# The output projection's weight rests subtracted on GpSimd instead of VectorE

## The chip, the cores and the metric

The kernel runs on one core of a Trainium2 chip. A core has five engines that run side by side, each with its own order of instructions: TensorE multiplies matrices, VectorE and ScalarE work on rows of up to 128 partitions, GpSimd does general work and sums over partitions, SyncE issues transfers. They wait for each other through semaphores. The metric is the device time of one execution in microseconds, as the median of several.

## The reference

One layer of a decoder, for a prompt of 1024 tokens and for eight samples with one new token each, whose keys and values of 2048 earlier tokens lie in a cache of pages of 128. All in 32-bit floating point. The middle part is what matters here:

```
o = attend(q, k, v, lam)                      # differential attention, 4 heads
o = rmsnorm(o, subln_g) * (1 - lam_init)
pz, pool_state = pool(z)                      # causal pooling, windows 2/4/8/16
m = concatenate([o, pz]) @ w_out              # the output projection, 1024 x 1024
x = x + g1 * rmsnorm(m, post_mix_g)
```

For the samples, the attention weights are a softmax over the 2048 cached positions and the new one, in two halves per head: exp(l - max) / sum, and the second half is subtracted with the factor `lam`. Ahead of this stand the adaptive modulation and the input projection; behind it a router and 64 experts, of which each token uses eight.

## The kernel before

The program is a row of stages with a barrier between them. In the first (up to 344 us) the input is projected, and the scores of the samples against all 128 pages of cached keys are left in `sc`, 128 partitions by 1088 columns. The stage of interest runs from 344 to about 730 us; behind it come router and experts.

This stage has 32 items: 8 blocks of 128 prompt tokens by 4 heads (`s` = 4 `i` + `k`). Each engine runs through the items in an order written out by hand. For an item, TensorE makes the scores (L1278, L1282), VectorE takes the maxima (L1453), ScalarE the exponentials (L1089), VectorE combines the two softmaxes (L1462 to L1467), TensorE transposes (L1308), ScalarE copies out (L1098), TensorE multiplies with the values (L1317), and VectorE copies the result into `o_h` (L1475). The scores of item s+1 are made ahead of item s's transposes.

Two further things are woven into the first items.

*The samples' weights.* VectorE takes the maximum of `sc` over pages (L1586, semaphore `dmax`); GpSimd takes the maximum over partitions (L1070, `gmax`); in item 0 VectorE subtracts it (L1603) and ScalarE takes the exponential (L1196); in item 1 VectorE sums over pages (L1607, `dsum`); GpSimd sums over partitions (L1072, `gsum`); in item 2 VectorE makes the weights `wV` from this (L1527 to L1538). From item 3 on TensorE multiplies 11 pages of values per item with `wV` (L1295). The pages come through a ring of seven buffers, `vring`; SyncE issues a page once the page seven places ahead of it has been used.

*The output projection's weights.* The projection is done with three products of rounded numbers: each operand is split in a rounded part and a rest. `w_raw` (1024 x 1024, eight blocks of 128 x 1024) is loaded at the start of the stage. In items 0 to 3 ScalarE rounds two blocks each into `w_hi` (L1200, semaphore `w_hi_made`), and VectorE subtracts them into `w_lo` (L1613, `w_lo_made`), which lies in the place of `w_raw`. TensorE uses them for the first time in item 4 (L1339), behind a wait for all eight rests.

GpSimd has little else in this stage: behind the two sums over partitions it makes the 16 small biases of the norms (L1063, L1067), the first of them near 419 us.

Of the kernel before, what the change touches and what calls it, by code (L numbers as in the profile page):

```python
# [8 lines left out]
F32 = mybir.dt.float32  # L9
# [3 lines left out]
ALU = mybir.AluOpType  # L13
# [6 lines left out]
KC = D // P  # L20
# [149 lines left out]
def build(nc, ins, outs):  # L170
# [7 lines left out]
    with ctx:  # L178
# [3 lines left out]
        def place(name, kb, shape, dt=F32):  # L182

            return nc.alloc_sbuf_tensor_at(name, shape, dt, offset=base + int(kb * 1024))
# [3 lines left out]
        def sem(name, keep=False):  # L188
            s = nc.alloc_semaphore(name)
            if not keep:  # L190
                used.append(s)
            return s
# [667 lines left out]
        W_STEPS = 4  # L860
# [39 lines left out]
        w_raw = place("w_raw", 139, [P, KC, D])  # L900
        w_lo = place("w_lo", 139, [P, KC, D], F32R)
        w_hi = place("w_hi", 171, [P, KC, D], F32R)
# [13 lines left out]
        w_hi_made, w_lo_made = sem("w_hi_made"), sem("w_lo_made")  # L916
# [29 lines left out]
        with nc.Block() as block:  # L946
# [112 lines left out]
            @block.gpsimd  # L1059
            def _(pool):  # L1060
                def bias_m(i):
                    pool.wait_ge(ss_m, 2 * i + 2)
                    pool.tensor_scalar(s3[:, 2:3], s3[:, 1:2], 1.0 / D, EPS, ALU.mult, ALU.add).then_inc(m_bias, 1)  # L1063

                def bias_x(i):
                    pool.wait_ge(ss_x, 2 * i + 2)
                    pool.tensor_scalar(s3[:, 6:7], s3[:, 5:6], 1.0 / D, EPS, ALU.mult, ALU.add).then_inc(x_bias, 1)  # L1067

                pool.wait_ge(dmax, 1)
                pool.partition_all_reduce(dm[:, 1, :], dm[:, 0, :], P, RED.max).then_inc(gmax, 1)  # L1070
                pool.wait_ge(dsum, 1)
                pool.partition_all_reduce(dm[:, 3, :], dm[:, 2, :], P, RED.add).then_inc(gsum, 1)  # L1072
                for i in range(1, NT):
                    bias_m(i - 1)
                    if i >= 2:
                        bias_x(i - 2)
                bias_x(NT - 2)
                bias_m(NT - 1)
                bias_x(NT - 1)
# [366 lines left out]
            def _(dve):  # L1446
                own = Own(dve, dve2)

                def maxima(s):
                    i = s // NH  # L1450
                    for m in range(2):
                        dve.wait_ge(s_done[m], s + 1)
                        dve.tensor_reduce(s2[s % 4][:, m:m + 1],  # L1453
                                          ps[:, 2 * m:2 * m + 2, :].rearrange("p b t -> p (b t)")[:, 0:(i + 1) * P], AX_X,
                                          ALU.max, negate=True).then_inc(nmax_here[m], 1)

                def combine(s):

                    st_, n = s2[s % 4], (s // NH + 1) * P
                    for m in range(2):  # L1460
                        dve.wait_ge(exp_done[m], s + 1)
                    own(dve.reciprocal(st_[:, 4:6], st_[:, 2:4]))  # L1462
                    own.wait()
                    own(dve.scalar_tensor_tensor(out=st_[:, 6:7], in0=st_[:, 2:3], scalar=neglam[:, 0:1], in1=st_[:, 5:6],
                                                 op0=ALU.mult, op1=ALU.mult))
                    own.wait()
                    dve.scalar_tensor_tensor(out=ex2[s % 2][0][:, 0:n], in0=ex2[s % 2][1][:, 0:n], scalar=st_[:, 6:7],  # L1467
                                             in1=ex2[s % 2][0][:, 0:n], op0=ALU.mult, op1=ALU.add).then_inc(w_made, 1)

                def o_copy(s):  # L1470
                    i, h = s // NH, s % NH
                    dve.wait_ge(pv_done, s + 1)
                    if h == 0 and i:
                        dve.wait_ge(oT_tr, i)
                    dve.tensor_scalar(o_h[:, h, :], ps[:, 6, 0:P], s2[s % 4][:, 4:5], None, ALU.mult).then_inc(o_here, 1)  # L1475
# [9 lines left out]
                def rest_attended(i):  # L1485
                    dve.wait_ge(hi_att, i + 1)
                    dve.scalar_tensor_tensor(out=mix_lo[:, 0:NH, :], in0=ps[:, 4, :].rearrange("p (h t) -> p h t", t=P),
                                             scalar=subln[:, 0:1], in1=mix_hi[:, 0:NH, :].bitcast(F32), op0=ALU.mult,
                                             op1=ALU.subtract).then_inc(lo_att, 1)
# [35 lines left out]
                def decode_weights():  # L1525
                    dve.wait_ge(gsum, 1)
                    own(dve.reciprocal(dm[:, 0, :], dm[:, 3, :]))  # L1527
                    own.wait()
                    r = dm[:, 0, :].rearrange("p (s h m) -> p s h m", s=NS, m=2)
                    own(dve.tensor_scalar(r[:, :, :, 1], r[:, :, :, 1], neglam[:, 0:1], None, ALU.mult))  # L1530
                    own.wait()
                    e = sc.rearrange("p s g (h m) -> p s g h m", m=2)
                    own(dve.tensor_tensor(wV[:, :, :, :], e[:, :, :, :, 0],
                                          r[:, :, :, 0].unsqueeze(2).to_broadcast([P, NS, NPG + 1, NH]), ALU.mult))
                    own(dve.tensor_tensor(wtmp[:, :, :, :], e[:, :, :, :, 1],
                                          r[:, :, :, 1].unsqueeze(2).to_broadcast([P, NS, NPG + 1, NH]), ALU.mult))
                    own.wait()
                    dve.tensor_tensor(wV[:, :, :, :], wV[:, :, :, :], wtmp[:, :, :, :], ALU.add).then_inc(wv_made, 1)  # L1538
# [49 lines left out]
                for s in range(NI):  # L1588
                    i, k = s // NH, s % NH
                    if s == 20:  # L1590
                        dve.wait_ge(od_tr, 1)
                        dve.tensor_scalar(msr[:, 0:NH, :], ps[:, 7, 0:NS * NH].rearrange("p (s h) -> p h s", h=NH), subln[:, 0:1],
                                          None, ALU.mult).then_inc(od_here, 1)
                    if s:
                        o_copy(s - 1)
                    if k == 1 and i >= 1:
                        rest_attended(i - 1)
                    combine(s)
                    if s + 1 < NI:
                        maxima(s + 1)  # L1600
                    if s == 0:
                        dve.wait_ge(gmax, 1)
                        dve.tensor_tensor(sc[:, :, :, :], sc[:, :, :, :],  # L1603
                                          dmv[:, 1].unsqueeze(2).to_broadcast([P, NS, NPG + 1, HM]), ALU.subtract).then_inc(sc_sub, 1)
                    if s == 1:
                        dve.wait_ge(sc_exp, 1)
                        dve.tensor_reduce(dmv[:, 2], by_page, AX_X, ALU.add).then_inc(dsum, 1)  # L1607
                    if s == 2:
                        decode_weights()
                    if s < W_STEPS:  # L1610
                        for c8 in (2 * s, 2 * s + 1):
                            dve.wait_ge(w_hi_made, c8 + 1)
                            dve.tensor_tensor(w_lo[:, c8, :], w_raw[:, c8, :], w_hi[:, c8, :].bitcast(F32), ALU.subtract  # L1613
                                              ).then_inc(w_lo_made, 1)
                    if s == 17:
                        samples_attended()
                    if s == 21:
                        dve.wait_ge(msh_made, 1)
                        dve.tensor_tensor(msl[:, :, :], msr[:, :, :], msh[:, :, :].bitcast(F32), ALU.subtract).then_inc(msl_made, 1)
                    if s == 28:  # L1620
                        samples_squared()
                    if s == 18:
                        samples_scaled()
                    if k == 0 and i >= 1:
                        o_norm(i - 1)
                    if k == 0 and i >= 3:
                        second_norm(i - 3)
                    if k == 1 and i >= 3:
                        shifted(i - 3)
                    if k == 1 and i >= 2:  # L1630
                        first_norm(i - 2, m_sb[:, :])
                    if s == 29:
                        samples_first()
                    if k == 2 and i >= 2:
                        residual(i - 2)
                    if k == 3:
                        rest_pooled(i)
# [1030 lines left out]
```

## Time and profile before

| what | value |
|---|---|
| median of 3 runs | 1836.78 us (1835.76 to 1837.87) |
| profiled execution | 1837.63 us |
| its span, first to last instruction | 1835.9 us |
| TensorE busy | 1682.7 us (92%) |
| VectorE busy | 1132.3 us (62%) |
| ScalarE busy | 888.6 us (48%) |
| GpSimd busy | 654.7 us (36%) |
| the stage of interest | 344 to about 730 us |

The profile is of one execution. Busy shares are means over stages with different limits: TensorE's 92% over the span hides that it is busy for half of the time in the first 24 us of the stage of interest. The trace below the page gives single instructions with start and duration, and for the idle time ahead of one what ended it. Matmul rows are drawn together when they follow each other, and their ends are modelled.

### The profile page before, as it was taken

What the parts mean: (1) busy time and instruction counts of PE and PEld (TensorE: products, weight loads), DVE (VectorE), ACT (ScalarE), POOL (GpSimd) and SP (SyncE); (2) the same over time, 40 slices, a digit from 0 to 9 for tenths busy, and PEclk for the clock granted to TensorE, in tenths of its full rate; (3) what the DMA queues carried; (4) which work ended last, traced back from release to release, by engine and by line L of the source; (5) the groups of instructions that cost most, each with busy time, mean ns of one, the idle gap of its engine ahead of it and who ended that gap; (6) DMA issues with size and microseconds to landing.
All of it is one profiled execution on the core that took longest, in us unless ns stands there. A gap on an engine that the chain in (4) does not pass through costs nothing.

```text
span 1835.9 us, 25633 instructions
## 1 busy us (share of the span) xinstructions
PE 1682.7 (92%) x8473; PEld 1208.1 (66%) x8474; DVE 1132.3 (62%) x1511; ACT 888.6 (48%) x1325; POOL 654.7 (36%) x555
## 2 busy tenths in 40 slices
PE   5999999598988998685999999999999999999995
PEld 3555555333356667264888888888888888888842
DVE  3255665532235555655777777777777777777627
ACT  1011111233345554134766666667667766666623
POOL 0056677200000000104555555555555555555300
PEclk8999999699998999797999999999999999999998
DMA  9587866677752114636989989989999989989737
GB/s 337 199 284 271 280 212 213 237 216 224 242 200 69 69 46 178 255 124 242 297 286 311 303 288 311 310 295 306 303 308 310 293 306 314 291 300 326 227 129 252
DMA packets 151909, 457.38 MB, mean 249 GB/s; under 512 B 29592, under 2 KB 39794, under 8 KB 126169
## 3 DMA queue, kind: packets, MB, share of 16 engines
q1 hardware_dynamic: 111097, 368.08, 54.6%
q0 software_dynamic: 30720, 69.83, 16.7%
q10 hardware_dynamic: 9960, 17.83, 2.9%
q8 instruction: 68, 1.11, 0.2%
q14 instruction: 64, 0.52, 0.1%
HBM read 403.40 MB, written 86.54 MB: 267 GB/s over the span
## 4 chain that ended last, share of the span: by engine, by line
PE 51%; DVE 1%; DMA 1%; issue 1%; ACT 0%; POOL 0%; SPq 0%; ACTq 0%; POOLq 0%; DVEq 0%
PE ps L2231 28%; PE ps L2248 14%; PE ps L2217 5%; PE ps L2530 2%; PE ps L2255 1%; PE ps L2548 1%; DMA a<-acc_d 1%; DMA xg<-h_d,tokb 1%; DVE a L2598 0%; DVE lo_gu L2276 0%; DVE a L2601 0%; DVE a L2586 0%; DVE xT_lo L2280 0%; DVE lo_dn L2276 0%; POOL xg L2140 0%
## 5 line engine op out<-in xcount | busy, mean ns | idle before, releaser
L2231 PE MATMUL ps<-hi_gu,xT_hi 128*128 128x512 f32 x768 | 309.2, 403 | 0.0
L2276 DVE TENSOR_TENSOR lo_gu<-raw_gu,hi_gu 128x1024 fp32r<-128x1024 f32 x256 | 304.1, 1219 | 4.5
L2231 PE MATMUL ps<-hi_gu,xT_lo 128*128 128x512 f32 x768 | 300.7, 392 | 0.0
L2231 PE MATMUL ps<-lo_gu,xT_hi 128*128 128x512 f32 x768 | 298.9, 389 | 0.0
L2170 ACT ACTIVATE hi_gu<-raw_gu 128x1024 fp32r<-128x1024 f32 x256 | 260.6, 1064 | 0.0
L2134 POOL DMA_INDIRECT acc_d<-yb,tokb x96 | 227.9, 2374 | 43.3 <-ACT yb L2184 28.3
L2115 POOL DMA_INDIRECT xg<-h_d,tokb x96 | 101.8, 1060 | 368.1 <-PE ps L2217 366.9
L602 PE MATMUL ps<-w_in_sb,hT 128*128 128x512 f32 x512 | 226.4, 600 | 1.1 <-ACT hT L466 1.1
L446 POOL TENSOR_TENSOR prod<-kring,qbc 128x512 f32<-128x512 f32 x128 | 160.1, 1279 | 176.6 <-DMA kring<-in_cache_k 125.1
L602 PEld LDWEIGHTS ps<-w_in_sb,hT 128*128 128x128 f32 x512 | 97.0, 192 | 119.3 <-issue 118.0
L2184 ACT ACTIVATE yb<-ps,wslot 128x1024 f32<-128x1024 f32 x96 | 107.0, 1115 | 137.7 <-PE ps L2248 137.7
L2231 PEld LDWEIGHTS ps<-hi_gu,xT_lo 128*128 128x128 f32 x768 | 144.2, 188 | 32.1
L2231 PEld LDWEIGHTS ps<-lo_gu,xT_hi 128*128 128x128 f32 x768 | 144.9, 189 | 27.9
L2231 PEld LDWEIGHTS ps<-hi_gu,xT_hi 128*128 128x128 f32 x768 | 144.7, 188 | 26.5
L2280 DVE TENSOR_TENSOR xT_lo<-ps,xT_hi 128x1024 fp32r<-128x1024 f32 x96 | 117.5, 1224 | 71.2 <-ACT xT_hi L2176 71.2
L2276 DVE TENSOR_TENSOR lo_dn<-raw_dn,hi_dn 128x1024 fp32r<-128x1024 f32 x128 | 153.4, 1219 | 2.3
L2248 PE MATMUL ps<-hi_dn,hT_hi 128*128 128x512 f32 x384 | 149.5, 389 | 1.7 <-DVE hT_lo L2301 1.7
L2248 PE MATMUL ps<-hi_dn,hT_lo 128*128 128x512 f32 x384 | 150.7, 392 | 0.0
L2248 PE MATMUL ps<-lo_dn,hT_hi 128*128 128x512 f32 x384 | 149.4, 389 | 0.0
L756 DVE TENSOR_REDUCE sc<-prod 128x8 f32<-128x512 f32 x128 | 86.6, 684 | 84.8 <-POOL prod L446 83.8
L2301 DVE TENSOR_TENSOR hT_lo<-ps,hT_hi 128x256 fp32r<-128x256 f32 x96 | 40.8, 425 | 150.1 <-ACT hT_hi L2207 150.1
L2170 ACT ACTIVATE hi_dn<-raw_dn 128x1024 fp32r<-128x1024 f32 x128 | 132.3, 1064 | 0.0
(343 smaller groups left out, 2611.1 us busy)
## 6 DMA issues: line engine op xcount, KB each, us to landing
raw_gu<-in_expert_w_gate SPq DMA_DIRECT2D x64, 1024.0 KB, 8.3
raw_gu<-in_expert_w_up SPq DMA_DIRECT2D x64, 1024.0 KB, 12.0
raw_dn<-in_expert_w_down SPq DMA_DIRECT2D x64, 1024.0 KB, 7.4
kring<-in_cache_k SPq DMA_DIRECT2D x128, 256.0 KB, 3.3
vring<-in_cache_v SPq DMA_DIRECT2D x128, 256.0 KB, 3.0
adaw<-in_ada_w ACTq DMA_DIRECT2D x7, 2048.0 KB, 13.0
adaw<-in_ada_w SPq DMA_DIRECT2D x5, 2048.0 KB, 16.0
w_in_sb<-in_w_in SPq DMA_DIRECT2D x4, 2048.0 KB, 20.8
```

The source lines that it names most:

```text
L446: pool.tensor_tensor(prod[g % 2][:, :], kring[g % 4][:, :], qbc[n % 2][:, :], ALU.mult).then_inc(prod_made, 1)
L602: m = pe.matmul(ps[:, bank, :], hT[:, k, :], w_in_sb[:, k, col * AW:(col + 1) * AW], start=(k == 0), stop=(k == KC - 1))
L756: dve.tensor_reduce(sc[:, p // NPG, p % NPG, :], prod[p % 2].rearrange("p (m d) -> p m d", d=HD), AX_X, ALU.add).then_inc(prod_read, 1)
L2115: pool.indirect_dma_start(out=xg[b % 2][:, :], out_offset=None, in_=h2_d[:, :], in_offset=bass.IndirectOffsetOnAxis(ap=tokb[:, b:b + 1], a ...
L2134: pool.indirect_dma_start(out=acc_d[b % 2][:, :], out_offset=bass.IndirectOffsetOnAxis(ap=tokb[:, b:b + 1], axis=0), in_=yb[b % 2][:, :], ...
L2170: act.activation(hi_cut(n, u), raw_cut(n, u), ACT.Copy).then_inc(hi_made, 1)
L2184: act.activation(yb[b % 2][:, :], ps[:, 4 + 2 * (b % 2):6 + 2 * (b % 2), :].rearrange("p b n -> p (b n)"), ACT.Copy, scale=wslot[b % 4][:, ...
L2217: last = pe.transpose(ps[:, k // 4, (k % 4) * P:(k % 4 + 1) * P], xg[b % 2].rearrange("t (p k) -> t k p", k=KC)[:, k, :], ident)
L2231: last = pe.matmul(ps[:, 2 + b % 2, :].rearrange("p (a f) -> p a f", a=2), x[b % 2][:, k, :], w[:, :, k * F:(k + 1) * F], start=(k == 0 an ...
L2248: last = pe.matmul(ps[:, 4 + 2 * (b % 2) + half, :], h[b % 2][:, ch, :], w[:, ch, cols], start=(ch == 0 and h is hT_hi and w is wh), stop= ...
L2276: dve.tensor_tensor(lo_cut(n, u), raw_cut(n, u), hi_cut(n, u).bitcast(F32), ALU.subtract).then_inc(lo_made, 1)
L2280: dve.tensor_tensor(xT_lo[b % 2].rearrange("p k t -> p (k t)"), ps[:, 0:2, :].rearrange("p b n -> p (b n)"), xT_hi[b % 2].bitcast(F32).rea ...
```

## The change

The four places in VectorE's items 0 to 3 at which it subtracts two blocks go. GpSimd subtracts the first two blocks between its two sums over partitions, and the other six behind the second sum, ahead of the biases. The waits stay the same: a block is subtracted once it is rounded, and TensorE waits for all eight. Line numbers of the changed kernel are up to 10 higher.

```
                 pool.wait_ge(dmax, 1)
                 pool.partition_all_reduce(dm[:, 1, :], dm[:, 0, :], P, RED.max).then_inc(gmax, 1)
+                rest_of_w(0, 2)
                 pool.wait_ge(dsum, 1)
                 pool.partition_all_reduce(dm[:, 3, :], dm[:, 2, :], P, RED.add).then_inc(gsum, 1)
+                rest_of_w(2, KC)
...
+                def rest_of_w(first, end):
+                    for c8 in range(first, end):
+                        pool.wait_ge(w_hi_made, c8 + 1)
+                        pool.tensor_tensor(w_lo[:, c8, :], w_raw[:, c8, :], w_hi[:, c8, :].bitcast(F32), ALU.subtract
+                                           ).then_inc(w_lo_made, 1)
...
                     if s == 2:
                         decode_weights()
-                    if s < W_STEPS:
-                        for c8 in (2 * s, 2 * s + 1):
-                            dve.wait_ge(w_hi_made, c8 + 1)
-                            dve.tensor_tensor(w_lo[:, c8, :], w_raw[:, c8, :], w_hi[:, c8, :].bitcast(F32), ALU.subtract
-                                              ).then_inc(w_lo_made, 1)
```

```order
143 L1070 ISA
144 L1070 ISA dm<-dm 128x64
145 L1072 ISA dm<-dm 128x64
146 L1063 ISA
147 L1063 TENSOR_SCALAR s_4652<-s_4652 128x1 x2
148 L1067 TENSOR_SCALAR s_4652<-s_4652 128x1
```

The same place of the changed kernel:

```order
143 L1076 ISA
144 L1076 ISA dm<-dm 128x64
145 L1072 ISA
146 L1072 TENSOR_TENSOR w_lo<-w_raw,w_hi 128x1024 x2
147 L1079 ISA
148 L1079 ISA dm<-dm 128x64
149 L1072 ISA
150 L1072 TENSOR_TENSOR w_lo<-w_raw,w_hi 128x1024 x6
151 L1063 TENSOR_SCALAR s_4652<-s_4652 128x1 x2
```

Two subtractions have come between the two sums and six behind them, and the bare ISA rows have become four.

VectorE from the subtraction of the maximum (item 0) to the weights of the samples (item 2), before. `s_...` are the item's small columns, `ex_...` its exponentials:

```order
L1603 TENSOR_TENSOR sc<-sc,dm 128x1088
L1613 TENSOR_TENSOR w_lo<-w_raw,w_hi 128x1024 x2
L1475 TENSOR_SCALAR o_h<-ps,s_4647 128x128
L1462 RECIPROCAL s_4648<-s_4648 128x2
L1464 SCALAR_TENSOR_TENSOR s_4648<-s_4648,neglam 128x1
L1467 SCALAR_TENSOR_TENSOR ex_10_4624<-ex_11_4625,s_4648,ex_10_4624 128x128
L1453 TENSOR_REDUCE s_4649<-ps 128x1 x2
L1607 TENSOR_REDUCE dm<-sc 128x64
L1613 TENSOR_TENSOR w_lo<-w_raw,w_hi 128x1024 x2
L1475 TENSOR_SCALAR o_h<-ps,s_4648 128x128
```

The same place of the changed kernel:

```order
L1611 TENSOR_TENSOR sc<-sc,dm 128x1088
L1483 TENSOR_SCALAR o_h<-ps,s_4647 128x128
L1470 RECIPROCAL s_4648<-s_4648 128x2
L1472 SCALAR_TENSOR_TENSOR s_4648<-s_4648,neglam 128x1
L1475 SCALAR_TENSOR_TENSOR ex_10_4624<-ex_11_4625,s_4648,ex_10_4624 128x128
L1461 TENSOR_REDUCE s_4649<-ps 128x1 x2
L1615 TENSOR_REDUCE dm<-sc 128x64
L1483 TENSOR_SCALAR o_h<-ps,s_4648 128x128
```

The subtractions are gone from between the score work and the copies into `o_h`; the rest keeps its order.

## Rows read from the trace of the kernel before

**Rows 1.** The page's chain that ended last: engine, tile, line, share of the span.

```profile
PE 51%; DVE 1%; DMA 1%; issue 1%; ACT 0%; POOL 0%; SPq 0%; ACTq 0%; POOLq 0%; DVEq 0%
PE ps L2231 28%; PE ps L2248 14%; PE ps L2217 5%; PE ps L2530 2%; PE ps L2255 1%; PE ps L2548 1%; DMA a<-acc_d 1%; DMA xg<-h_d,tokb 1%; DVE a L2598 0%; DVE lo_gu L2276 0%; DVE a L2601 0%; DVE a L2586 0%; DVE xT_lo L2280 0%; DVE lo_dn L2276 0%; POOL xg L2140 0%
```

**Rows 2.** Stretches of the stage: length, busy time per engine, clock, DMA share, GB/s.

```profile
core 0: us, PE busy (x) PEld busy (x) DVE busy (x) ACT busy (x) POOL busy (x), PEclk, DMA share, GB/s
344.00:368.00 24.00, 13.18 (x47) 9.09 (x48) 17.33 (x33) 12.49 (x31) 1.26 (x2) 0.50 0.85 319
368.00:374.00 6.00, 5.23 (x21) 0.94 (x20) 3.88 (x9) 2.74 (x10) 0.00 (x0) 0.50 0.32 89
374.00:376.00 2.00, 2.00 (x7) 0.68 (x6) 1.98 (x2) 1.45 (x2) 0.00 (x0) 0.62 0.78 213
376.00:387.00 11.00, 10.57 (x35) 1.97 (x32) 2.78 (x8) 3.42 (x9) 0.00 (x0) 1.00 0.73 229
387.00:420.00 33.00, 30.31 (x141) 14.58 (x141) 6.42 (x19) 9.25 (x27) 0.24 (x1) 1.00 0.80 245
420.00:450.00 30.00, 26.18 (x95) 7.88 (x95) 4.99 (x12) 7.01 (x18) 0.00 (x0) 1.00 0.76 234
```

**Rows 3.** Waits in 344 to 387 us: in total, times, longest.

```profile
PEld ps L1295 <- DMA vring<-in_cache_v: 5.5, 6, 1.2
```

**Rows 4.** TensorE's timeline: start, us, line, operation, idle time before and what ended it.

```profile
358.87 0.47 PE L1308 MATMUL ps<-const,ex 128*128 128x128 f32 x1 [3.79 <-DVE ex L1467]
...
364.81 0.48 PE L1308 MATMUL ps<-const,ex 128*128 128x128 f32 x1 [2.42 <-DVE ex L1467]
...
367.53 1.22 PE L1282 MATMUL ps<-const 128*128 128x128 f32 x4
368.68 1.89 PE L1295 MATMUL ps<-vring,wV 128*4 128x512 f32 x8
371.34 0.48 PE L1308 MATMUL ps<-const,ex 128*128 128x128 f32 x1 [0.77 <-DVE ex L1467]
...
386.88 0.50 PE L1339 MATMUL ps<-w_hi,mix_hi 128*128 128x512 f32 x1
```

**Rows 5.** GpSimd's whole timeline from 340 to 425 us.

```profile
350.80 0.54 POOL L1070 PARTITION_ALL_REDUCE dm<-dm  x1 [11.96 <-issue]
361.33 0.72 POOL L1072 PARTITION_ALL_REDUCE dm<-dm  x1 [9.99 <-DVE dm L1607]
419.28 0.24 POOL L1063 TENSOR_SCALAR s<-s 128x1 f32<-128x1 f32 x1 [57.23 <-ACT junk L1142]
```

**Rows 6.** VectorE's timeline in items 0 to 2.

```profile
344.11 2.04 DVE L1586 TENSOR_REDUCE dm<-sc 128x64 f32<-128x1088 f32 x1
...
352.08 1.28 DVE L1603 TENSOR_TENSOR sc<-sc,dm 128x1088 f32<-128x1088 f32 x1
...
357.76 0.34 DVE L1475 TENSOR_SCALAR o_h<-ps,s 128x128 f32<-128x128 f32 x1
...
365.07 0.54 DVE L1527 RECIPROCAL dm<-dm 128x64 f32<-128x64 f32 x1
...
367.32 0.72 DVE L1538 TENSOR_TENSOR wV<-wV,wtmp 128x544 f32<-128x544 f32 x1
```

**Rows 7.** Groups of 344 to 387 us: busy us, mean ns, idle time before, releaser.

```profile
L1613 DVE TENSOR_TENSOR w_lo<-w_raw,w_hi 128x1024 fp32r<-128x1024 f32 x8 | 9.5, 1230 | 4.3 <-ACT w_hi L1200 4.2
```

**Rows 8.** ScalarE's timeline: the first two roundings, the releaser of GpSimd's first bias.

```profile
354.41 1.99 ACT L1200 ACTIVATE w_hi<-w_raw 128x1024 fp32r<-128x1024 f32 x2
...
418.99 0.19 ACT L1142 ACTIVATION_READ_ACCUMULATOR junk<-m_sb 128x1 f32 x1
```

**Rows 9.** Instructions of L1070 and L1063: duration in ns, first and last start.

```profile
L1070 POOLq MODIFY_POOL_CONFIG  x2: 11/11/11, 344.0 to 344.0; - x2
...
L1063 POOLq MODIFY_POOL_CONFIG  x2: 88/88/88, 362.0 to 362.0; - x2
```

**Rows 10.** GpSimd's groups of the whole span, by shape.

```profile
L446 POOL TENSOR_TENSOR prod<-kring,qbc 128x512 f32<-128x512 f32 x128 | 160.1, 1279 | 176.6 <-DMA kring<-in_cache_k 125.1 <-DVE sc L756 50.7
L1770 POOL TENSOR_TENSOR sg<-sg,gu_sb 128x256 f32<-128x256 f32 x2 | 1.5, 760 | 21.5 <-ACT sg L1798 21.5
```

## The prediction

> **What bounds the kernel now.** The chain that ended last [rows 1] runs for 28% of the span through one matmul line of the experts, far behind the change, so it says nothing about a change at 350 us. What counts is whether the stage that holds the change ends earlier or later, because all engines meet at a barrier behind it and a shift there reaches the end undiminished. So I read the stage in stretches [rows 2]. Until 368 TensorE is busy for 13.18 of 24 us at its lower clock: a chain of dependences sets the pace, with VectorE the fullest engine (17.33 us). From 376 on TensorE is busy for 10.57 of 11 us and then 30.31 of 33 us, at its higher clock. In between it takes the cached value pages in order, and what it waits for there is the page loads [rows 3], which themselves wait for pages to be used up. Whatever moves the first matmul on a page therefore moves everything behind it. That matmul is the point to compute: 368.68 before [rows 4].
>
> It needs the weights `wV`, and these need the second sum over partitions. Before, the sum itself did not hold them back: it ran at 361.33 [rows 5], while VectorE came to the weights only at 365.07, in its own order, and finished at 367.32 + 0.72 = 368.04 [rows 6]. TensorE was still at the scores of item 4 until 368.7 [rows 4] and waited for nothing.
>
> **VectorE's part.** Eight subtractions leave it, 9.5 us of work, with 4.2 us of waits for ScalarE's rounding [rows 7]. What that frees is real: before, TensorE stood 3.79 and 2.42 us for VectorE's combination of items 1 and 2 [rows 4], and both waits came from the two subtractions queued ahead. Without them the copy of item 0 starts at 353.4, when the score subtraction ends (352.08 + 1.28), not at 357.76 [rows 6]. ScalarE rounds weights until 354.41 + 1.99 = 356.40 [rows 8] and turns item 1 right behind, some 2.5 us sooner; item 2 gains as much again. TensorE would be through item 4's scores near 363.5, some 5 us earlier. It then meets the first value page, and that needs the second sum. This gain is kept only if GpSimd delivers the sum by about 360.5.
>
> **GpSimd's part: the loads.** Order shows more than eight subtractions: a bare ISA row stands ahead of every change between a sum over partitions and ordinary arithmetic. Before there are two, now four, and three of them matter: ahead of the first two subtractions, ahead of the second sum, ahead of the last six. In the trace these rows are MODIFY_POOL_CONFIG [rows 9]. Ahead of the first sum it stands at 344.0, the sum's input is ready at 344.11 + 2.04 = 346.15 [rows 6], and the sum starts at 350.80 [rows 5]: 6.8 us after the row, 4.65 us after its input, with idle time for which the profile finds no releaser. The second sum, with no such row ahead, starts within 0.1 us of its input. So a change towards the sums costs between 4.65 us (if it is paid when the first call comes) and 6.8 us (if it runs from the row on), or nothing where only the first load of a program costs. I take 6.8, the whole gap of the only row that shows one.
>
> The way back was hidden before: row at 362.0 [rows 9], the next operation at 419.28, 0.10 us after its input (418.99 + 0.19) [rows 5, 8]. That excludes a toll on the first call behind its wait; a load of anything up to 57 us from the row on is still possible, and so is none. I take the same 6.8.
>
> The Trainium skill, "GPSIMD Engine Reference", section 2.1, says that the first call to a freshly loaded library pays a load of about 6 us (5.95). The trace agrees in size, its 4.65 and 6.8 lying on either side. With 5.95 for each load from the row on, the sum below would come to +2.9, an estimate of 1839.7; with 5.95 paid behind each wait, to +7.0 and 1843.8.
>
> **GpSimd's part: the subtractions.** No row has 128x1024 on GpSimd. 128x256 takes 760 ns and 128x512 takes 1279 [rows 10]; the straight line gives 1279 + 512 x 2.03 = 2.32 us, twice the larger row gives 2.56. I take 2.32. VectorE did one in 1.23 [rows 7], so the work itself grows.
>
> The Trainium skill, "GPSIMD Engine Reference", section 4.1, tells the reader to keep elementwise work on VectorE, since GpSimd is about twice as slow with two inputs. The rows agree (2.32 against 1.23). By that rule alone the two subtractions ahead of the sum would cost 2.2 us more, and the sum without any loads would still end ahead of before.
>
> **The sum**, from the end of the first sum at 350.80 + 0.54 = 351.34:
> - load back: 358.14. The first two rounded blocks are there at 356.40, so they do not decide.
> - two subtractions, 4.64: 362.78
> - load for the sums, 6.80: 369.58. The input of the second sum, with VectorE relieved, is ready near 357.5 and does not decide.
> - second sum, 0.72: 370.30
> - VectorE's weights, 368.04 - 365.07 = 2.97: 373.27
>
> The first page's matmul stands at 373.3 instead of 368.68: **+4.6 us**. TensorE waits some 10 us for it, and VectorE, standing at the same semaphore, holds back the copy and combination of items 2 and 3; these are late by as much, but ready before TensorE has done its four pages. Before, TensorE lost 0.77 us there [rows 4]; I count no gain from that, since page 7 lands a fixed time after page 0 is used.
>
> Next are the last six rests, which TensorE first reads in item 4's output projection at 386.88 [rows 4], now 391.5. Load back 370.30 + 6.80 = 377.10; six subtractions, 13.9: 391.0. That is in time by only 0.5 us. With 2.56 each, the first page moves to +5.1 and the rests come at 392.9 against 392.0, together +6.1.
>
> The clock: it was at its lower level until 374, and went up in the stretch from 374 to 376 [rows 2], when TensorE had run nearly without a gap since 368. It now stands idle for 10 us ahead of the pages. If the rise comes as long after the first page as before, nothing changes; if it comes up to 2 us later than that, those 2 us run at half speed and cost at most 1 us, less what the page waits hide. I take 0.3.
>
> Behind 392 TensorE is busy some nine tenths of the time [rows 2] and its other waits are for partners that wait for it, so nothing gives the shift back. In all +4.9 us. On the profiled execution (1837.63 us, span 1835.9) that is 1842.5; it lies 0.85 above the median, and against the median of 1836.78 it is **1841.7 us**.
>
> **Rivals.**
> - *The way is short.* Either only the change towards the sums costs, or each load is nearer to 4.65. One way: subtractions from 355.5, when the first block is rounded, to 360.1, load, sum and weights end at 368.5 to 370.6, and the first page at 0 to +2.0. Both ways at 4.65 from the row: +0.3. Both at 6.3: +3.6. So 1836.8 to 1840.4. For it: the direction back shows no toll, and the first load ran while the DMA engines were filling up (share 0.85 [rows 2]); a quieter time may be kinder. Against: the gap of 6.8 is the one that was seen. Chance 0.27.
> - *Loads cost only once* (faster). If the 6.8 us was a matter of the first use, the second sum runs at 360.2, the weights end at 363.9, and the first page, with TensorE ready at 363.5, stands 4.7 us earlier: 1832.1. It decides from a second load below 1 us. Against it: the row itself is there again each time. Chance 0.11.
> - *The way back is longer than the way out.* With 10 us, the first subtraction starts at 361.3, the first page comes at +7.8, and the last six rests end at 397.4 against TensorE's 394.7: +10.5, 1847.3. Nothing in the trace excludes it, nothing shows it. Chance 0.10.
>
> **How the numbers follow.** The forecast, both loads near 6.8, gets 0.52, with a range of its own from 1840.5 to 1844. What a measurement of this kernel can tell from no change is about 0.2%, 3.7 us. Faster by that: 0.11, the one-time load. Within it: 0.27, the short way. Slower: 0.52 + 0.10 = 0.62. The range leaves out the faster rival and the far end of the long one: 1836 to 1847.
>
> **What would show it.** In the profile after: four MODIFY_POOL_CONFIG places; the first rest on GpSimd near 358.1 (355.5 if the way back is free), at 2.3 us each; the second sum near 369.6; VectorE's reciprocal of the sums right behind with some 10 us of idle time ahead; TensorE's first page near 373.3 with as long a wait; the last rest near 391 and no wait, or one below 1 us, in the first output projection. Wrong would be a second sum near 360 (loads only once), a first rest far behind 358 (long way back), subtractions clearly above 2.6 us, or a stage behind 392 that wins back the shift, through the page loads or an earlier clock.

## The result and the profile after

The change makes the kernel slower. The median is 1845.09 us (1836.08 to 1851.17, 18 runs) against 1836.47 us (1831.56 to 1840.45, 18 runs); the ratio is 1.0048, with a 95% interval from 1.0035 to 1.0061, that is some 9 us (6 to 11). Executions of one kernel spread over several microseconds, and the profiled one of the changed kernel, 1836.08 us with a span of 1834.3, happens to be its shortest. So positions are told here as us into the stage, counted from SyncE's first issue in it: 344.01 in the profile before, 341.33 in the profile after.

GpSimd's timeline at the start of the stage, after (start, duration, line, operation, and in brackets the idle time ahead):

```profile
347.43 0.54 POOL L1076 PARTITION_ALL_REDUCE dm<-dm  x1 [11.28 <-issue]
359.22 4.63 POOL L1072 TENSOR_TENSOR w_lo<-w_raw,w_hi 128x1024 fp32r<-128x1024 f32 x2 [11.25 <-ACT w_hi L1208]
369.58 0.73 POOL L1079 PARTITION_ALL_REDUCE dm<-dm  x1 [5.73 <-issue]
377.17 14.50 POOL L1072 TENSOR_TENSOR w_lo<-w_raw,w_hi 128x1024 fp32r<-128x1024 f32 x6 [6.86 <-issue]
```

Where [rows 5] had two sums with nothing between, three idle times now stand: 11.25 us behind the first sum, 5.73 ahead of the second, 6.86 behind it. The first is put down to ScalarE's rounding, but that was done long before, as ScalarE's timeline shows:

```profile
351.67 1.99 ACT L1208 ACTIVATE w_hi<-w_raw 128x1024 fp32r<-128x1024 f32 x2
```

Both blocks were ready at 353.66, and GpSimd began at 359.22. The loads answer to [rows 9] in the instructions of L1072 and L1079:

```profile
L1072 POOLq MODIFY_POOL_CONFIG  x4: 98/98/98, 347.9 to 370.3; - x4
...
L1079 POOLq MODIFY_POOL_CONFIG  x2: 1/1/1, 364.1 to 364.1; - x2
```

They stand at the head of each idle time. VectorE and TensorE, answering to [rows 6] and [rows 4]:

```profile
352.59 2.10 DVE L1615 TENSOR_REDUCE dm<-sc 128x64 f32<-128x1088 f32 x1
...
370.35 0.55 DVE L1535 RECIPROCAL dm<-dm 128x64 f32<-128x64 f32 x1 [13.19 <-POOL dm L1079]
```

```profile
359.29 1.22 PE L1290 MATMUL ps<-const 128*128 128x128 f32 x4
373.39 1.89 PE L1303 MATMUL ps<-vring,wV 128*4 128x512 f32 x8 [12.88 <-DVE wV L1546]
...
391.72 0.50 PE L1347 MATMUL ps<-w_hi,mix_hi 128*128 128x512 f32 x1 [0.20 <-POOL w_lo L1072]
```

The gain ahead is there: the second sum's input is ready at 354.69, and TensorE is through the scores of item 4 at 360.5, 19.2 us into the stage instead of 24.7. Then VectorE stands for 13.19 us and TensorE for 12.88. The first value page comes 32.06 us into the stage instead of 24.67, the output projection 50.39 instead of 42.87: 7.4 and 7.5 us late.

The stretches that answer to [rows 2]; the first two are counted from the start of the stage in this profile, so that they cover the same parts of it as there:

```profile
341.33:365.33 24.00, 13.40 (x49) 9.39 (x49) 10.29 (x23) 12.32 (x31) 5.18 (x3) 0.50 0.85 319
365.33:371.33 6.00, 0.00 (x0) 0.00 (x0) 0.91 (x3) 0.00 (x0) 0.73 (x1) 0.50 0.00 0
...
376.00:387.00 11.00, 9.99 (x32) 1.84 (x26) 6.06 (x7) 3.71 (x9) 9.83 (x4) 0.85 0.77 216
```

In the first 24 us of the stage VectorE's work has fallen from 17.33 to 10.29 us, and in the 6 us behind them no engine works for more than 0.91 us, while before TensorE worked for 5.23.

The stage's end is seen at the first operation of the next one on GpSimd: 747.54 before and 746.91 after, or 403.5 and 405.6 us into the stage. So in this one execution 5 us of the shift were won back behind item 4. The stretch from the first matmul of the first output projection to that operation, before and after:

```profile
386.88:747.54 360.66, 314.39 (x1604) 196.20 (x1603) 149.10 (x258) 154.16 (x360) 4.53 (x17) 0.94 0.47 154
```

```profile
391.72:746.91 355.19, 307.88 (x1603) 192.06 (x1603) 149.04 (x258) 153.28 (x360) 4.18 (x16) 0.96 0.48 156
```

The shorter stretch ran at a mean granted clock of 0.96 instead of 0.94. In all eight profiles of this document it takes 354.6 to 361.7 us, whatever the version: the three below 358 us at 0.95 or 0.96, the five above 359 at 0.93 or 0.94. The changed kernel stands on both sides, with 355.19 here and 359.78 in the next run, so what was won back here goes with the clock of this execution. Why the clock differs between executions is not shown.

### The profile page after: what moved, and what is told of

Read it like the earlier page. It is cut to its first block, busy times and chain, and to the rows that moved or that the text cites. A ratio compares the mean times of both kernels' runs of the same rounds, so it can differ in the third digit from the quotient of the medians.

```text
span 1834.3 us, 25637 instructions
## 1 busy us (share of the span) xinstructions
PE 1673.2 (91%) x8473; PEld 1202.8 (66%) x8474; DVE 1128.6 (62%) x1503; ACT 887.5 (48%) x1325; POOL 673.9 (37%) x563
## 4 chain that ended last, share of the span: by engine, by line
PE 51%; DMA 1%; DVE 1%; issue 1%; ACT 0%; POOL 0%; SPq 0%; ACTq 0%; POOLq 0%; DVEq 0%
PE ps L2234 29%; PE ps L2251 14%; PE ps L2220 5%; PE ps L2533 2%; PE ps L2258 1%; PE ps L2551 1%; DMA a<-acc_d 1%; DMA xg<-h_d,tokb 0%; DVE a L2601 0%; DVE a L2604 0%; DVE a L2589 0%; POOL xg L2143 0%; ACT hT L2501 0%; DVE a L2583 0%; DVE xT_lo L2283 0%
```

## The experiments

A load that leads from the sums back to ordinary arithmetic is called a way back here, one towards the sums a way out.

Theory A: the three loads on GpSimd set the shift, through the second sum and the first value page. Against it stand: the first way back was long by chance (B); the subtractions' own length or their sharing of memory with VectorE (C); the first page doesn't set the stage (D).

**The changed kernel once more.** No edit.

> The changed kernel once more, for a second profile beside the first. Times are told from the start of the stage (344.0 us in the profile before, 341.3 in the profile after). Theory A (loads): the three loads on GpSimd are there again, the way out to the sums near 6 us, the first way back longer than the second one (11.3 and 6.9 in the first profile), the first value page near 32 us into the stage against 24.7 before, and the time 6 to 11 us above before. Theory B (the first profile was a chance): the first way back comes out near 7, the first page near 28 to 29, and the time about 5 us above before.

1.0051 (1.0034 to 1.0068). GpSimd's timeline (the stage starts at 342.97):

```profile
363.35 4.63 POOL L1072 TENSOR_TENSOR w_lo<-w_raw,w_hi 128x1024 fp32r<-128x1024 f32 x2 [12.93 <-issue]
374.00 0.73 POOL L1079 PARTITION_ALL_REDUCE dm<-dm  x1 [6.01 <-issue]
382.01 14.49 POOL L1072 TENSOR_TENSOR w_lo<-w_raw,w_hi 128x1024 fp32r<-128x1024 f32 x6 [7.28 <-issue]
```

The first way back is long again, 12.93 us, and here the trace names no releaser. TensorE's first page and first projection:

```profile
377.80 1.89 PE L1303 MATMUL ps<-vring,wV 128*4 128x512 f32 x8 [15.59 <-DVE wV L1546]
...
396.55 0.50 PE L1347 MATMUL ps<-w_hi,mix_hi 128*128 128x512 f32 x1 [0.56 <-POOL w_lo L1072]
```

That is 34.83 and 53.58 us into the stage, 10.2 and 10.7 later than before. The next stage begins here at 413.4 us into the stage, 9.8 later than before: nearly the whole shift arrives. B falls, since the first way back is long in both profiles, and the page came later than the 32 us that I had expected. The page is late by 7.4 and 10.2 us in two executions, which agrees with the 9 us between the times.

**The loads without the subtractions.** VectorE keeps all of its work; GpSimd adds one column between the sums:

```diff
+        small_done = sem("small_done")
...
                 pool.partition_all_reduce(dm[:, 1, :], dm[:, 0, :], P, RED.max).then_inc(gmax, 1)
+                pool.wait_ge(gmax, 1)
+                pool.tensor_tensor(dm[:, 0, 0:1], dm[:, 0, 0:1], dm[:, 0, 0:1], ALU.add).then_inc(small_done, 1)
                 pool.wait_ge(dsum, 1)
+                pool.wait_ge(small_done, 1)
```

> The kernel before, with VectorE doing all subtractions as before, and one addition of a single column on GpSimd between the two sums, so that the two loads come in without any subtraction moving. Theory A (loads set the shift): way back 7 to 11 us, way out near 6, the second sum at 21 to 25 us into the stage instead of 17.3, the first value page at 25 to 28.5 instead of 24.7, and the time 1 to 4 us above before, near 1840. Theory C (the subtractions' own length on GpSimd, or their sharing of memory with VectorE, sets the shift): the second sum within 1 us of before and no change in time.

1.0025 (1.0013 to 1.0036), 4.6 us slower. GpSimd (the stage starts at 344.15) and TensorE:

```profile
362.91 0.97 POOL L1073 TENSOR_TENSOR dm<-dm 128x1 f32<-128x1 f32 x1 [11.38 <-issue]
369.82 0.73 POOL L1076 PARTITION_ALL_REDUCE dm<-dm  x1 [5.93 <-issue]
```

```profile
373.62 1.89 PE L1299 MATMUL ps<-vring,wV 128*4 128x512 f32 x8 [4.81 <-DVE wV L1542]
```

An addition of one column takes 0.97 us and costs 11.38 ahead and 5.93 behind. The first page comes at 29.47, 4.8 late, a little above the bound of 28.5 us that theory A had named. C asked for no change and falls as the main cause. The changed kernel comes another 2.6 to 5.4 later: its two subtractions, 4.63 us, stand in line with the loads.

**All eight behind the second sum.** No load stands between the sums:

```diff
-                rest_of_w(0, 2)
...
-                rest_of_w(2, KC)
+                rest_of_w(0, KC)
```

> The changed kernel with all eight subtractions behind the second sum, so that no load stands between the two sums. Theory A: the second sum at about 13.5 us into the stage, the first value page at 19.5 to 20 instead of 24.7 (5 us earlier than before), then one load back of 7 to 11 us from about 14.5, eight subtractions of 2.33 us, the last at 40 to 44.5, and TensorE, at the first output projection near 38, waits 2 to 6 us for it: in all between 3 us faster and 1 us slower than before, 1833 to 1838. Theory C: the subtractions slow VectorE down beside them and the time stays 4 us or more above before.

1.0021 (1.0006 to 1.0035): slower, beyond the range that I had given. GpSimd (the stage starts at 344.78) and TensorE:

```profile
368.24 19.55 POOL L1072 TENSOR_TENSOR w_lo<-w_raw,w_hi 128x1024 fp32r<-128x1024 f32 x8 [9.24 <-issue]
```

```profile
364.37 2.75 PE L1302 MATMUL ps<-vring,wV 128*4 128x512 f32 x8
...
378.29 0.44 PE L1315 MATMUL ps<-const,ex 128*128 128x128 f32 x2 [0.27 <-DVE ex L1474]
...
387.84 0.79 PE L1346 MATMUL ps<-w_hi,mix_hi 128*128 128x512 f32 x1 [5.47 <-POOL w_lo L1072]
...
393.06 0.61 PE L1324 MATMUL ps<-v_all,wtsT 128*128 128x128 f32 x4
```

The first page is at 19.59, 5.1 us earlier than before, as A says. Then one load of 9.24 and 19.55 us of subtractions end at 43.0, and TensorE stands 5.47 us: the whole lead is lost at the output projection (43.06 against 42.87). What I had not counted is the clock. Stretches around that wait:

```profile
380.80:384.80 4.00, 1.57 (x6) 0.09 (x2) 1.53 (x2) 2.04 (x3) 4.00 (x2) 1.00 0.89 250
384.80:388.80 4.00, 0.96 (x2) 0.83 (x3) 0.79 (x1) 0.00 (x0) 2.99 (x2) 0.67 0.74 246
388.80:392.80 4.00, 4.00 (x11) 3.06 (x10) 0.00 (x0) 0.00 (x0) 0.00 (x0) 0.50 0.05 17
```

TensorE was busy 1.57 and 0.96 of 4 us, its clock fell from the higher to the lower level, and the projection behind ran at that: 0.79 us for its first matmul, 0.50 in [rows 4]. From the first matmul of the projection to the one behind it, it took 5.22 us; in the kernel before it took 2.89, from 386.88 to this row:

```profile
389.77 0.60 PE L1317 MATMUL ps<-v_all,wtsT 128*128 128x128 f32 x4
```

The 2.3 us between them are part of the 3.9 by which this version is slower (1 to 6 by the interval); for the rest nothing is shown. The number alone would fit theory C too. Its cause doesn't: TensorE stood only 0.27 us for VectorE's late combination, and 5.47 for the subtractions themselves.

**All eight on VectorE, but late.** No load is added, and VectorE isn't relieved:

```diff
-                    if s < W_STEPS:
-                        for c8 in (2 * s, 2 * s + 1):
+                    if s in (2, 3):
+                        for c8 in ((0, 1), range(2, KC))[s - 2]:
```

> The kernel before with the subtractions left on VectorE, but two of them in item 2 and six in item 3, behind the weights of the samples, none in items 0 and 1. No load is added. Theory A (the first value page sets the stage): the page at 19.5 to 20 us into the stage instead of 24.7, the last rest at about 32, in time for the output projection near 38; 4 to 5 us faster than before, near 1832. Theory D (the stage behind the first page is held by something else, page loads or stores): the page is earlier by 5 us and the time is the same.

0.9971 (0.9958 to 0.9984), 5.3 us faster than before (3 to 8 by the interval); the fastest of all versions here. VectorE and TensorE (the stage starts at 344.62):

```profile
367.32 6.89 DVE L1613 TENSOR_TENSOR w_lo<-w_raw,w_hi 128x1024 fp32r<-128x1024 f32 x6
```

```profile
363.88 2.91 PE L1295 MATMUL ps<-vring,wV 128*4 128x512 f32 x8
...
381.77 0.50 PE L1339 MATMUL ps<-w_hi,mix_hi 128*128 128x512 f32 x1
```

The page is at 19.26 and the projection at 37.15, 5.4 and 5.7 us earlier, with the rests done at 29.6. D falls: the first page does set the stage, as long as the rests are there for the projection, and what was wanted, to take the subtractions out of the way of items 0 and 1, needs no other engine.

**The first way back with transfers held.** SyncE issues half of the weights and the queries, and then waits for the first rest:

```diff
                 for j in range(2):
                     sp.dma_start(w_raw[:, 4 * j:4 * j + 4, :], wv[:, 4 * j:4 * j + 4, :]).then_inc(w_here[j], 16)
-                load_q(1)
+                    if j == 0:
+                        load_q(1)
+                        sp.wait_ge(w_lo_made, 1)
```

> The changed kernel, but SyncE, after the first half of the projection's weights and the second block of queries, waits for the first rest before it issues the other loads of this stage (second half of the weights, pooled part, x, router weights, value pages). So the transfers fall quiet while GpSimd makes its first way back. Theory A1 (a load is slowed by other transfers: 11.3 and 12.9 us with the transfer engines full, 6.9 and 7.3 with them nearly idle): the first way back now takes 6.5 to 8 us, the first rest starts at 13.5 to 15.5 us into the stage instead of 17.9 and 20.4, the second sum at 24 to 27. Theory A2 (the first way back is long by itself): 11 to 13 us again, with no other transfer beside it. The time of the whole is no test here, since the held loads come late: between 1836 and 1850.

1.0061 (1.0038 to 1.0083); as said, the time is no test of the theories. GpSimd (the stage starts at 341.59):

```profile
355.95 4.70 POOL L1074 TENSOR_TENSOR w_lo<-w_raw,w_hi 128x1024 fp32r<-128x1024 f32 x2 [7.27 <-ACT w_hi L1210]
370.75 0.73 POOL L1081 PARTITION_ALL_REDUCE dm<-dm  x1 [10.10 <-issue]
378.17 14.52 POOL L1074 TENSOR_TENSOR w_lo<-w_raw,w_hi 128x1024 fp32r<-128x1024 f32 x6 [6.69 <-issue]
```

With few transfers beside it (share 0.22 of full, rows at the end) the way back takes 7.27 us, not 11 to 13; and the way out, into which the held transfers now fall, takes 10.10 instead of 5.7 to 6.0. A load is lengthened by transfers beside it, in either direction (A1). The second sum came at 29.2, later than expected for that reason.

**Four on GpSimd behind the sums, four on VectorE in item 3.**

```diff
-                rest_of_w(0, 2)
...
-                rest_of_w(2, KC)
+                rest_of_w(0, 4)
...
+                    if s == 3:
+                        for c8 in range(4, KC):
+                            dve.wait_ge(w_hi_made, c8 + 1)
+                            dve.tensor_tensor(w_lo[:, c8, :], w_raw[:, c8, :], w_hi[:, c8, :].bitcast(F32), ALU.subtract
+                                              ).then_inc(w_lo_made, 1)
```

> No subtraction between the sums; GpSimd takes blocks 0 to 3 behind the second sum, VectorE blocks 4 to 7 in item 3. Theory A: the first page at 19.5 us into the stage; GpSimd's four between about 23.5 and 33, VectorE's four by 33; TensorE does not wait at the projection near 38, and the time is that of the version with all eight late on VectorE, 1830 to 1833. Theory E (VectorE, with two inputs in SBUF, is held while GpSimd works: 1.85 instead of 0.22 us and 2.53 instead of 0.48 in the other runs): VectorE's four take 2 us and more each, the combination of item 4 comes late, and 1 to 4 us of the gain are lost, 1832 to 1836.

0.9996 (0.9985 to 1.0007), the same as before. VectorE (the stage starts at 342.74) and TensorE:

```profile
363.13 2.35 DVE L1620 TENSOR_TENSOR w_lo<-w_raw,w_hi 128x1024 fp32r<-128x1024 f32 x2
368.66 4.54 DVE L1620 TENSOR_TENSOR w_lo<-w_raw,w_hi 128x1024 fp32r<-128x1024 f32 x2 [3.18 <-ACT w_hi L1207]
373.12 2.83 DVE L1500 TENSOR_TENSOR mix_lo<-mixp,mix_hi 128x512 fp32r<-128x512 f32 x1
...
376.32 1.85 DVE L1471 SCALAR_TENSOR_TENSOR s<-s,neglam 128x1 f32<-128x1 f32 x1
```

```profile
378.74 0.44 PE L1315 MATMUL ps<-const,ex 128*128 128x128 f32 x2 [2.31 <-DVE ex L1474]
...
383.91 0.80 PE L1346 MATMUL ps<-w_hi,mix_hi 128*128 128x512 f32 x1
```

GpSimd works from 366.49 to 378.15. VectorE's first two subtractions, ahead of that, take 2.35 us together; the next two, beside it, 4.54. Two operations behind them take 2.83 and 1.85 us, where the version with all eight late on VectorE shows 0.69 and 0.22. These delays add up to some 6 us, more than the 2.31 us that TensorE then waits for item 4's combination. VectorE also stood 3.18 us for ScalarE's rounding of the last blocks; by these numbers the combination would, without the delays, have been there before TensorE asked for it in spite of that (an estimate). The clock falls here too, in the stretch behind the wait:

```profile
374.70:378.70 4.00, 1.71 (x4) 0.09 (x2) 3.93 (x6) 0.40 (x2) 3.45 (x2) 1.00 0.78 244
378.70:382.70 4.00, 3.96 (x9) 0.48 (x12) 0.65 (x2) 1.79 (x6) 0.00 (x0) 0.63 0.80 232
```

So of the lead at the first page, 5.0 us, only 1.7 is left at the projection (41.17 against 42.87). Theory E holds: help from GpSimd costs VectorE, and by its wait TensorE's clock, about what it gives.

## Why the prediction was right in kind and short in size

The forecast was +4.9 us with a range from 1836 to 1847; measured were 8.6 us between the medians, and 1845.09 lies in the range. Slower had 0.62. The sum, term by term, in the two profiles of the changed kernel:

| term | forecast | profile after | second profile |
|---|---|---|---|
| first way back | 6.80 | 11.25 | 12.93 |
| two subtractions | 4.64 | 4.63 | 4.63 |
| way out to the sums | 6.80 | 5.73 | 6.01 |
| second sum | 0.72 | 0.73 | 0.73 |
| weights | 2.97 | 2.98 | 2.98 |
| first page later by | 4.6 | 7.4 | 10.2 |
| second way back | 6.80 | 6.86 | 7.28 |
| six subtractions | 13.9 | 14.50 | 14.49 |
| TensorE's wait at the projection | 0 | 0.20 | 0.56 |

- **The mechanism was right**: the bare ISA rows as loads paid every time, the straight line between two smaller shapes for the subtractions (2.32 us), VectorE and TensorE standing for the second sum, the last rests arriving within a microsecond of their use.
- **One term was mis-sized: the first way back.** I took the one gap that the trace showed, 6.8 us, and priced the way back like the way out. It takes 11 to 13 us, 4.5 to 6.1 more, and that is nearly the whole miss; the way out was shorter by about 1. I had seen that the first load ran while the transfers were still filling up, and concluded that later ones might be shorter. The first way back lies in the fullest stretch of all, and the profile before could have shown it (the stretch from 351 to 362 us, with the transfer share as the number before the last):

```profile
351.00:362.00 11.00, 6.48 (x26) 4.60 (x25) 8.12 (x13) 7.00 (x17) 1.01 (x2) 0.50 1.04 393
```

- **The rival of a longer way back** had the right effect with the wrong cause. It made every way back long; the second one, in a quiet stretch, took 6.86 and 7.28.
- **A toll on the first call, or loads only once**: both fall. Every further row brought a further idle time. And a load does not wait for the input of its first call: the first sum of the profile after has its input at 343.48, 2.1 us behind its row, and starts at 347.43, only 3.95 us later, while the shortest whole load here took 5.73.
- **The clock** cost nothing here: 0.3 us was allowed. The stretch from 376 to 387 us at 0.85 holds some 3.3 us at the lower level, so the rise came about 6 us behind the first page; before it was about 7. From the first page to the projection it is 18.3 and 18.8 us in the two profiles, the wait for the rests included, and 18.2 before. It did cost in the two versions in which TensorE had to wait in the midst of its pages, which I had not foreseen.
- **The other signs**: the second sum near 369.6, first rest near 358, were meant for a stage that begins at 344.0; set into the stage they read 25.6 and 14.1, and came at 28.25 and 17.89.
- **"Nothing gives the shift back"** held in the second profile within 1 us. In the first, 5 us of it were gone by the end of the stage, with a higher granted clock; the forecast had no term for this spread between executions.

## What to carry to other kernels

Before moving work to GpSimd, look in the order of its instructions for changes of library: each is paid again, in the order in which they stand, and two kinds of work that alternate there cost two loads for every turn. Count such a load by the stretch in which it will run and by how full the transfer engines are in it, not by the one row that happens to show it. If an engine is in the way of a chain, first ask whether its work can stand later on the same engine: here that gave 5.3 us, where moving it lost 9.

## What the runs showed of the hardware

**The length of a load follows the transfers beside it.** The stretch from a sum's or a subtraction's end to the next operation's start, its length and, as the last two numbers, transfer share and GB/s. Profile after, in the order first way back, way out, second way back:

```profile
347.97:359.22 11.25, 8.92 (x33) 6.01 (x33) 6.95 (x17) 9.44 (x26) 0.00 (x1) 0.50 1.03 394
363.85:369.58 5.73, 0.00 (x0) 0.00 (x0) 0.00 (x0) 0.00 (x0) 0.00 (x1) 0.50 0.00 0
370.31:377.17 6.86, 3.78 (x15) 0.40 (x15) 4.45 (x11) 1.85 (x8) 0.00 (x1) 0.50 0.11 24
```

With the transfers held, first way back and way out:

```profile
348.68:355.95 7.27, 5.30 (x22) 3.60 (x21) 5.97 (x14) 6.08 (x17) 0.01 (x1) 0.50 0.22 72
360.65:370.75 10.10, 1.80 (x8) 0.93 (x4) 0.00 (x0) 2.00 (x2) 0.00 (x1) 0.50 1.03 399
```

All eight behind the second sum, the one way back:

```profile
359.00:368.24 9.24, 8.88 (x33) 4.01 (x34) 5.85 (x17) 6.00 (x17) 0.00 (x1) 0.64 0.88 318
```

The way out takes 5.73 us with no transfers and 10.10 among full ones, the way back 6.7 to 7.3 us among few and 11 to 13 among full ones, with 9.24 in between. The Trainium skill, "GPSIMD Engine Reference", section 2.1, gives about 6 us for such a load; the ways out with few transfers agree (5.73 to 6.01), the loads among full ones (10.10 to 12.93) don't, and the measurement decides.

**VectorE is held while GpSimd works, if it reads two operands from SBUF.** VectorE's timeline in items 4 and 5 of the changed kernel, the first beside the six subtractions:

```profile
380.38 0.15 DVE L1470 RECIPROCAL s<-s 128x2 f32<-128x2 f32 x1
380.57 1.71 DVE L1472 SCALAR_TENSOR_TENSOR s<-s,neglam 128x1 f32<-128x1 f32 x1
382.31 2.54 DVE L1475 SCALAR_TENSOR_TENSOR ex<-ex,s,ex 128x256 f32<-128x256 f32 x1
...
399.14 0.22 DVE L1472 SCALAR_TENSOR_TENSOR s<-s,neglam 128x1 f32<-128x1 f32 x1
399.39 0.48 DVE L1475 SCALAR_TENSOR_TENSOR ex<-ex,s,ex 128x256 f32<-128x256 f32 x1
```

The last two rows are the same operations one item later, with GpSimd idle: 0.22 and 0.48 us. Beside the subtractions they take 1.71 and 2.54; the reciprocal, which reads one operand, is as fast as ever (0.15, and 0.16 one item later). 2.54 us is about the length of one subtraction (2.42), as if the operation were let through between two of them; that is a reading, not shown. The Trainium skill, "GPSIMD Engine Reference", section 1, names contention of the two engines for SBUF when VectorE has two inputs there; these rows agree.

**TensorE's clock fell in the midst of the pages** in the two versions in which TensorE had to wait there: behind stretches with 1.57 and 0.96 of 4 us busy in the one, and with 1.71 in the other, it stood at the lower level (0.50 and 0.51 of full clock), in a place where the kernel before runs at the higher. Such a wait costs more than its length: the projection behind it took 2.3 us more in the first of the two. That the wait brought the fall about is read from their order; no run tests it apart.
